# Two-layer diffusion trunk: a ninth ring slot, another order of the first loads, and the last expert scattered by itself

## The reference

```python
h  = x * (1.0 + sc1) + sh1                        # the context tokens the same, with their own rows
a, b, c, gates = split(h @ w_in[l])               # w_in: 1024 x 4768; three kinds of attention and their gates
y  = (g_a * (o_a @ w_branch_a) + g_b * (o_b @ w_branch_b) + g_c * (o_c @ w_branch_c)) @ w_out
x  = layer_norm(ALPHA * x + g1 * y, ln1_g, ln1_b)
h  = x * (1.0 + sc2) + sh2
aff = softmax(h @ w_router)                       # 16 experts, each takes its 32 best tokens of a stream
hid = silu(xs @ w_gate[e]) * (xs @ w_up[e])       # three 1024 x 1024 matrices for each expert
y  = zeros.at[chosen].add((hid @ w_down[e]) * top_aff)
x  = layer_norm(ALPHA * x + g2 * y, ln2_g, ln2_b)
```

## Time and profile before

| | |
|---|---|
| time, median of 3 runs | 1828.52 us (1828.32 to 1828.54) |
| the profiled execution | 1827.84 us |
| its span, first to last instruction | 1826.0 us |
| PE busy | 1556.5 us, 85% |
| DVE, ACT, GpSimd busy | 492.2, 396.0, 26.0 us |
| moved by DMA | 522.82 MB, mean 286 GB/s |
| mean granted TensorE clock | 0.921 |

### The profile page before, as it was taken

The page is one execution under the profiler, slowest core; times in us unless marked ns, Lnnn a source line. Parts: engine busy times, 40 slices in busy tenths (PEclk is TensorE's granted clock), DMA queues, the critical chain, the costliest instruction groups (busy, mean ns, idle before and its releaser), DMA issues.

```text
span 1826.0 us, 23042 instructions
## 1 busy us (share of the span) xinstructions
PE 1556.5 (85%) x9700; PEld 812.4 (44%) x9700; DVE 492.2 (27%) x1063; ACT 396.0 (22%) x889; POOL 26.0 (1%) x49
## 2 busy tenths in 40 slices
PE   5999999999998998988888899899977766666665
PEld 1444446888654442423222356468644323332222
DVE  0124786333342000111010243865340000000002
ACT  1212667221221120100000132674221100000000
POOL 1000000000000000000000010000000000000000
PEclk8999999999998999999999899999979767778876
DMA  9435911333529899999999711026869999999995
GB/s 373 176 144 225 352 64 70 98 98 130 211 113 398 327 422 422 421 421 420 421 422 421 300 45 41 24 81 209 313 263 421 420 421 421 421 421 420 420 421 239
DMA packets 98038, 522.82 MB, mean 286 GB/s; under 512 B 10752, under 2 KB 12944, under 8 KB 42640
## 3 DMA queue, kind: packets, MB, share of 16 engines
q1 hardware_dynamic: 94384, 510.44, 69.6%
q0 software_dynamic: 3392, 10.85, 1.7%
q10 hardware_dynamic: 160, 0.06, 0.0%
HBM read 520.17 MB, written 1.15 MB: 285 GB/s over the span
## 4 chain that ended last, share of the span: by engine, by line
PE 56%; DMA 35%; DVE 6%; ACT 1%; issue 1%; POOL 0%; DVEq 0%; SPq 0%; ACTq 0%
PE psum L443 53%; DMA ring<-in_w_up 21%; DMA ring<-in_w_down 12%; PE psum L493 3%; DMA ring<-in_w_in 2%; DVE small L1515 1%; DMA ring<-in_w_ada 1%; DVE PR L1535 1%; ACT hT L1081 0%; DVE X L1630 0%; DVE X L1547 0%; DVE psum L1513 0%; DVE X L1546 0%; DVE small L1517 0%; DVE stats L1636 0%
## 5 line engine op out<-in xcount | busy, mean ns | idle before, releaser
L443 PE MATMUL psum<-ring,A 128*32 128x256 f32 (+2 forms) x3176 | 494.4, 538 | 127.1 <-DMA ring<-in_w_up 65.3
L443 PEld LDWEIGHTS psum<-ring,A 128*32 128x32 f32 (+2 forms) x3176 | 167.1, 138 | 425.3 <-issue 186.2
L443 PE MATMUL psum<-ring,PR 128*32 128x256 f32 (+1 forms) x1440 | 187.3, 506 | 44.5 <-DMA ring<-in_w_down 44.2
L443 PE MATMUL psum<-ring_r,h_hi 128*128 128x512 f32 x576 | 178.6, 392 | 5.8 <-DVE h_lo L1703 5.8
L443 PE MATMUL psum<-ring,hT 128*128 128x512 f32 (+2 forms) x512 | 171.5, 489 | 11.0 <-DMA ring<-in_w_in 5.3
L1666 DVE TENSOR_TENSOR W<-W,psum 128x512 f32<-128x512 f32 (+1 forms) x32 | 17.8, 555 | 557.4 <-PE psum L443 557.4
L443 PEld LDWEIGHTS psum<-ring,PR 128*32 128x32 f32 (+1 forms) x1440 | 62.5, 129 | 163.0 <-issue 79.1
L443 PEld LDWEIGHTS psum<-ring,hT 128*128 128x128 f32 x512 | 86.1, 194 | 83.2 <-issue 83.2
L443 PEld LDWEIGHTS psum<-ring_r,h_hi 128*128 128x128 f32 x576 | 108.7, 189 | 29.2 <-issue 6.6
L443 PE MATMUL psum<-ring_r,h_lo 128*128 128x512 f32 x288 | 112.6, 391 | 0.0
L1300 ACT ACTIVATE W<-psum 128x512 f32<-128x512 f32 (+1 forms) x32 | 15.7, 490 | 444.8 <-PE psum L443 444.8
(11 more groups left out here) (181 smaller groups left out, 1326.0 us busy)
## 6 DMA issues: line engine op xcount, KB each, us to landing
ring<-in_w_gate SPq DMA_DIRECT2D x125, 1024.0 KB, 17.8
ring<-in_w_up SPq DMA_DIRECT2D x124, 1024.0 KB, 17.8
ring<-in_w_down SPq DMA_DIRECT2D x120, 1024.0 KB, 17.9
ring<-in_w_ada SPq DMA_DIRECT2D x48, 1024.0 KB, 11.7
ring<-in_w_in SPq DMA_DIRECT2D x36, 1024.0 KB, 5.1
ring<-in_w_out SPq DMA_DIRECT2D x8, 1024.0 KB, 7.0
ring<-in_w_branch SPq DMA_DIRECT2D x8, 768.0 KB, 4.5
A<-in_w_down SPq DMA_DIRECT2D x4, 1024.0 KB, 6.1
```

What stands on the lines that cost most here:

```text
L443: return nc.tensor.matmul(o, a, b, start=start, stop=stop, skip_group_check=True)
```

## The change

- `RING` is 9. The slot's 8 KB in each partition come from the scratch for descriptors of GpSimd's DMAs, which is set to 8192 bytes.
- Of the tables SP loads only the identity ahead of `w_ada`; ACT loads the rest after its first `ada_move`. GpSimd issues `x`, and with it the parameters, when slot 1 has been filled twice, which is when piece 10 has landed.
- The 16 experts are scattered in groups of 4, 4, 4, 3 and 1 (`SCATTERS`). The three, for all tiles, stand before `down(15)`, and the last one after it. In layer 0 tile 3 of the last scatter takes banks 6 and 7.
- The parameters of the projection get places in `PR` and `W` that are free after the last down, and GpSimd loads them for layer 1 then, before the layer norms. In layer 1 DVE does P(1,0) ahead of H(2), and P(1,0) takes a bank in turn.

```diff
-RING, SLOT = 8, 2048
+RING, SLOT = 9, 2048
...
-DVE_FIRST = [("H", 2), ("H", 3), ("P", 1, 0), ("P", 1, 1)]
+DVE_FIRST = [("P", 1, 0), ("H", 2), ("H", 3), ("P", 1, 1)]
...
-SCATTER_AT = {8: 0, 10: 1, 13: 2}
+SCATTER_AT = {8: 0, 10: 1, 13: 2, 16: 3}
+
+SCATTERS = [4, 4, 4, 3, 1]
+LAST_BANKS = (6, 7)
...
-        uq = part(PR, 0, 2, 384)
-        ukv = part(PR, 768, 512)
-        gain_cq = part(PR, 1280, 384)
-        gain_q = part(PR, 1664, HD)
-        gain_k = part(PR, 1728, HD)
-        bias_rows, cin = part(PR, 3584, P)[0:48 * DEPTH, :], part(PR, 3712, P)[0:2 * KT, :]
+        uq = part(PR, 2560, 2, 384)
+        ukv = part(W, 3584, 512)
+        gain_cq = part(PR, 3328, 384)
+        gain_q = part(PR, 3712, HD)
+        gain_k = part(PR, 3776, HD)
+        bias_rows, cin = part(A, 0, P)[0:48 * DEPTH, :], part(A, 128, P)[0:2 * KT, :]
...
-                        b = begin(("P", l, ch, t), takers=2 if ch != 0 else 1,
-                                  bank=ADA_BANK if l and (ch, t) == (1, 0) else None)
+                        b = begin(("P", l, ch, t), takers=2 if ch != 0 else 1)
...
                 def scatter(g):
-                    pe.wait_ge(y_ready, EXPERTS * l + 4 * g + 4)
+                    pe.wait_ge(y_ready, EXPERTS * l + 4 * g + SCATTERS[g])
...
                     for ts in ([0, 2], [1, 3]) if G == 2 else (tiles(l),):
                         banks = scatter_banks(g, ts)
-                        for j in range(4):
+                        for j in range(SCATTERS[g]):
                             scatter_rows(g, j, ts, banks)
...
-                    if e == EXPERTS:
-                        pe.wait_ge(y_ready, EXPERTS * l + e - 1)
-                        first = tiles(l)[:2]
-                        banks = scatter_banks(3, first)
-                        for j in range(3):
-                            scatter_rows(3, j, first, banks)
                     if e >= 1:
                         down(e - 1)
                     if e < EXPERTS:
                         turn_hidden(e)
-                pe.wait_ge(y_ready, EXPERTS * l + EXPERTS)
-                scatter_rows(3, 3, first, banks)
-                for t in tiles(l)[2:]:
-                    banks = scatter_banks(3, [t])
-                    for j in range(4):
-                        scatter_rows(3, j, [t], banks)
+                if G == 2:
+                    banks = scatter_banks(4, [0, 1, 2]) | scatter_banks(4, [3], LAST_BANKS)
+                    pe.wait_ge(y_ready, EXPERTS * l + EXPERTS)
+                    scatter_rows(4, 0, [0, 2], banks)
+                    scatter_rows(4, 0, [1, 3], banks)
+                else:
+                    banks = scatter_banks(4, tiles(l))
+                    pe.wait_ge(y_ready, EXPERTS * l + EXPERTS)
+                    scatter_rows(4, 0, tiles(l), banks)
...
-            sp.dma_start(cst[:, :], consts).then_inc(consts_in, 16)
+            sp.dma_start(ident, consts[:, C_ID:C_ID + P]).then_inc(consts_in, 16)
...
-            pool.wait_ge(slot_filled[3], 16)
+            pool.wait_ge(slot_filled[1], 32)
             pool.dma_start(X[:, 2:4, :], x.rearrange("b (t p) d -> p (b t) d", p=P)).then_inc(x_in, 16)
...
                 if l:
-                    pool.wait_ge(x_ready, 2 * first_tile(l))
-                    for t in tiles(l - 1):
-                        for n in (0, 1):
-                            filled(pool, ("SC", l - 1, 3, t, n))
...
+                    filled(pool, ("YE", l - 1, EXPERTS - 1))
+                pool.dma_start(gain_cq[:, 0:256], row(b_q_norm[l, :])).then_inc(proj_par_in, 16)
+                pool.dma_start(gain_cq[:, 256:384], row(b_kv_norm[l, :])).then_inc(proj_par_in, 16)
+                pool.dma_start(uq, b_w_uq[l].rearrange("(j p) n -> p j n", p=P)).then_inc(proj_par_in, 16)
+                pool.dma_start(ukv, b_w_ukv[l]).then_inc(proj_par_in, 16)
...
+                if l:
+
                     for t in tiles(l - 1):
                         for n in (0, 1):
-                            filled(pool, ("SC", l - 1, 3, t, n))
+                            filled(pool, ("SC", l - 1, 4, t, n))
...
             ada_move(0, 0)
+            act.dma_start(cst[:, C_MASK:C_ALL], consts[:, C_MASK:C_ALL]).then_inc(tables_in, 16)
...
-                    for i, t in enumerate((0, 1, 2, 3) if g == 3 else (0, 2, 1, 3)):
+                    for i, t in enumerate((0, 1, 2, 3) if g == 4 else (0, 2, 1, 3)):
...
-    nc = bacc.Bacc("TRN2", target_bir_lowering=False, num_devices=1)
+    nc = bacc.Bacc("TRN2", target_bir_lowering=False, num_devices=1,
+                   dynamic_dma_scratch_size=8192)
```

More of the change, by code:

```diff
@@ L201, in trunk @@
         consts_in = sem("consts_in")
+        tables_in = sem("tables_in")
         c_in = sem("c_in")
@@ L824, in scatter_rows @@
                 def scatter_rows(g, j, ts, banks):
-                    e = 4 * g + j
+                    e, last = 4 * g + j, j == SCATTERS[g] - 1
+                    e = e - (g == 4)
                     for i in sorted({t % 2 for t in ts}):
@@ L833, in scatter_rows, with scatter_banks @@
                             ins = mm(psum[:, b, at:at + Wd], ohT[e // 8][row:row + CAP, e % 8, i * P:(i + 1) * P],
-                                     ysb[row:row + CAP, e % 8, 0:Wd], j == 0 and at == 0, j == 3)
-                            if j == 3 and (G == 2 or i == 1):
+                                     ysb[row:row + CAP, e % 8, 0:Wd], j == 0 and at == 0, last)
+                            if last and (G == 2 or i == 1):
                                 end(ins, b)
-                def scatter_banks(g, ts):
+                def scatter_banks(g, ts, held=None):
                     if G == 2:
-                        return {(t, n): begin(("SC", l, g, t, n)) for t in ts for n in range(G)}
+                        return {(t, n): begin(("SC", l, g, t, n), bank=held and held[n]) for t in ts for n in range(G)}
                     opened = [begin(("SC", l, g, n)) for n in range(G)]
@@ L1004, in _ @@
                 if l:
-                    pool.wait_ge(x_ready, 2 * first_tile(l))
+                    filled(pool, ("YE", l - 1, EXPERTS - 1))
[3 more added lines that the diff above has]
+                pool.dma_start(ukv, b_w_ukv[l]).then_inc(proj_par_in, 16)
+                pool.dma_start(gain_q, row(c_q_norm[l, :])).then_inc(proj_par_in, 16)
+                pool.dma_start(gain_k, row(c_k_norm[l, :])).then_inc(proj_par_in, 16)
+                pool.dma_start(sink[:, :], row(a_sink[l, :])).then_inc(sink_in, 16)
+                pool.dma_start(wr[:, :, :], w_router[l].rearrange("(k p) e -> p k e", p=P)).then_inc(router_in, 16)
+                if l:
                     for t in tiles(l - 1):
                         for n in (0, 1):
-                            filled(pool, ("SC", l - 1, 3, t, n))
-                pool.dma_start(uq, b_w_uq[l].rearrange("(j p) n -> p j n", p=P)).then_inc(proj_par_in, 16)
-                pool.dma_start(ukv, b_w_ukv[l]).then_inc(proj_par_in, 16)
-                pool.dma_start(gain_cq[:, 0:256], row(b_q_norm[l, :])).then_inc(proj_par_in, 16)
-                pool.dma_start(gain_cq[:, 256:384], row(b_kv_norm[l, :])).then_inc(proj_par_in, 16)
-                pool.dma_start(part(PR, 1664, HD), row(c_q_norm[l, :])).then_inc(proj_par_in, 16)
-                pool.dma_start(part(PR, 1728, HD), row(c_k_norm[l, :])).then_inc(proj_par_in, 16)
-                pool.dma_start(sink[:, :], row(a_sink[l, :])).then_inc(sink_in, 16)
-                pool.dma_start(wr[:, :, :], w_router[l].rearrange("(k p) e -> p k e", p=P)).then_inc(router_in, 16)
+                            filled(pool, ("SC", l - 1, 4, t, n))
                 nc.gpsimd.memset(qpad[:, :, :], 0.0).then_inc(pads_zero, 1)
@@ L1425, in qkv @@
                         b = second(dve, ("P", l, 3, t))
+                        if l == 0 and t == 2:
+                            dve.wait_ge(tables_in, 16)
                         if t < 2:
@@ L1642, in scatter @@
                             add_rows(("SC", l, g, n), slice(2, 4), slice(Wd * n, Wd * n + Wd))
-                        if g == 3:
+                        if g == 4:
                             for n in range(G):
@@ L1681, in experts @@
                         mark(bank_drained[b])
-                scatter(3)
+                scatter(4)
             dve.wait_ge(consts_in, 16)
```

2 lines of the change are left out of this document (1 added, 1 removed).

## The result

The changed kernel takes **1814.26 us** (median of 4 runs, 1812.56 to 1817.42) against 1828.53 (4 runs, 1828.32 to 1831.56): a ratio of 0.993, 95% interval 0.9918 to 0.9942. The forecast was 1815.4, so it came out 1.1 us from the median. The profiled execution took 1814.61 us with a span of 1812.8; the span before was 1826.0, so the two traces differ by 13.2 us, and this is the difference to be explained. That the sum came out near does not say that its terms did.

A forecast was written before the change was run, and what follows sets the result against it. The weight stream bounds both expert stages, PE the stretches between. 5.1 + 1.35 + 2.49 + 1.7 + 2.49 = 13.1 us off 1827.84 gives 1814.7; the median adds 0.68: 1815.4 us, range 1811.5 to 1821.5.

The forecast's parts named there:

- The turn: Between the layers, end of down(14) to P(1,2) of layer 1: regrouped scatters gain 1.7 us.
- the start: First loads of layer 0: transposes of x begin at 44.3 instead of 49.40 us, gaining 5.1 us (bounds 3.1 to 6.4).
- New on the path is x: At the start: x issued at 34.2, taking 10.0 us, lands at 44.3; PE waits 1.3 us.
- The w_ada product: After the last P(1,t) at 79.93 us: with nine slots piece 16 comes earlier, removing PE's wait of 1.35 us.
- The ring slot: Expert stages of layers 0 and 1: one more piece landed at each standstill, each ending 2.49 us sooner.
- 24 matmuls ahead of down(15), so 5.42 us more: At the turn: with about 0.5 us for the fifth bank, down(15) ends 5.9 us later.
- The early parameters and the order of DVE: Layer 1's early parameter loads and P(1,0) ahead of H on DVE: 0 beyond the rest, gain bound 0.7 us.
- A: Start: x is not waited for, start gains 6.4 us, in all 14.4, 1814.1 us; chance 0.08.
- B: Turn: the 5.9 us ahead of y(15) stay, total gain 5.5 us, 1823.0 us; chance 0.10.
- C: Expert stages: the ring slot is worth nothing, total gain 8.1 us, 1820.4 us; chance 0.10.
- D: Halved descriptor scratch: GpSimd has one load in flight, N(0) 9.9 us late, gain 3.2, 1825.3 us; chance 0.06.
- E: Expert stages: nine pieces in flight slow the stream below 421 GB/s; 3% loss gives +11 us, 1839; chance 0.06.

The follow-up runs named there:

- The start alone: Kernel before (eight slots) with only the new order of the first loads, x after piece 10: 1827.97 us, ratio 1.0001.
- the slot alone: Kernel before with nine ring slots and the smaller descriptor scratch, nothing else: 1821.77 us, ratio 0.9971.
- The pairs by stream: Changed kernel with layer 0's last two scatters over tiles (0,1), then (2,3): 1824.22 us, repeated 1819.28 us.
- the turn alone: Changed kernel with eight slots and the old order of the first loads: 1821.48 us, ratio 0.9965.
- the seven slots: Kernel before with seven ring slots instead of eight: 1840.2 us, ratio 1.0069.
- the third series: Runs on another chip than the first two series, with the changed kernel unaltered (1814.64 us) beside others; kernel before 1827.49 us.

## Why the forecast came out, term by term

The sum was right and two of its terms were not. The turn gave 3.8 us more than said and the start 4.4 us less, and that these nearly cancelled is luck.

**The start, 5.1 us: failed.** Product 7 came at 26.38 (25.6 said) and P(1,0) at 32.13 (33.0 said), so the first half of the argument held. The step that failed is "New on the path is x", with the wait for x that it puts at 1.3 us. It has three parts. x was issued 1.4 us later than said, at 35.58. It took 11.4 us and not 10.0, so it landed at 47.0, later than the 46 named as a sign of error. And PE, after waiting 4.32 us, ran at half clock for a while, 1.7 us more, which was in no term. 0.72 us came out, below my lower bound of 3.1. The start alone, 0.3 us in its trace and no difference in time, shows it by itself, and x issued three pieces earlier gives 6.57 us more at P(1,2) and 5.25 us in time. The estimate of 4.4 us for this load, worked out from the unit cost in the Trainium skill, DMA: Bandwidth & Descriptors, in its section on the anatomy of a DMA on the gpsimd path, was farther off than the row. No run here shows it: the load took 9.5 to 14.7 us in every place it was tried, beside the weight stream.

**The w_ada product, 1.35 us: right.** 1.43 us in the trace, and the wait is gone with the slot alone too. In that trace, though, only 0.2 us are left of it at 634 us, as P(1,0) ran slower there (9.93 us, 9.01 before).

**The ring slot, 2.49 us twice: right.** 2.88 and 2.59 us in the traces; with the slot alone 3.06 and 2.52. Both of the figures of layer 0 are taken from 634 us on, at a product that PE does not wait for, and are the looser ones. The reading "one piece for each slot" holds from eight to nine slots. From seven to eight it holds in layer 1 (2.26) and not in layer 0 (1.16).

**The turn, 1.7 us: right in direction, mis-sized.** The term of the sum that failed is "24 matmuls ahead of down(15), so 5.42 us more". I took 5.42 us for 12 matmuls from the earlier trace rows, where both tiles use the same rows; in the changed order they take 2.86. So the 24 matmuls add 2 x 2.86 + 1.45 (the bank wait, 0.5 said) - 5.42 = 1.75 us ahead of down(15) and not 5.9. The row with the right order stood in the same trace, at 795.13: by it the term is 1.6 us. The error was to price the matmuls by their shape and not by the order of the tiles. The pairs by stream, which restore that price alone, put P(1,0) at T+32.31 and cost 4.6 us. The Trainium skill, TensorE: Matmul & The Clock Gate, in Part 3 on packing small matmuls, has matmuls of 32 rows (K=32) whose operands lie in different 32-row groups run at the same time, and gives 3.07 times the speed as measured for four. The trace agrees in kind: from two groups to four it is 5.42/2.86 = 1.9 times. No run here shows the 3.07.

**The early parameters and the order of DVE, 0 beyond the above: right as a sum, wrong as a reading.** In the kernel before, DVE did its half of H(2) first, at 1069.99, and its share of P(1,0) only at 1072.55, when the parameters had just landed (1071.2); P(1,0) to P(1,2) took 22.4 us there, much as after. In the changed kernel with late loads they landed 23.6 us behind the start of P(1,0), hardly later than before (22.1), but now H(2) stands behind DVE's share of P(1,0) and waits with it: this costs 3.3 us up to P(1,2), and some 6 in the times. So what covered the late loads was DVE's old order and not the length of the turn. The early loads are no gain of their own but the condition for the new order. Whether DVE's new order is needed by itself was not tried: with P(1,0) no longer in a bank of its own, H(3) waits for the bank that DVE's share of P(1,0) drains, and the old order would have DVE do H(3) before it.

**The rivals.** A (x is not waited for): refuted, 4.32 us. B (the turn costs 5.9): refuted by the turn alone, which gives 6.1. C (the slot gives nothing in the expert stages): refuted by the slot alone and by the seven slots. D (GpSimd held to one load): refuted; it issued its nine loads 0.52 to 0.73 us apart, as before, PE did not wait at N(0) (58.50 us), and the slot alone, with the smaller scratch, lost nothing. E (a slower stream): refuted, 421 and 416 GB/s as before.

**The better version.** Every part of the change with x issued behind piece 7 takes 1809.39 to 1809.55 us against 1814.26 and 1814.64 for the changed kernel, and beats both kernels. The 5.2 us under the changed kernel are from the third series, where both ran side by side.

## What to carry to other kernels

Where a load is moved behind others to let them pass, the moved load is the new last arrival. Of the three places tried here the best was right behind the one piece that must not be delayed; one piece earlier and three pieces later were both worse. A wait can cost more than its length, since PE may run at half clock behind it. A ring slot in front of a stage bound by its stream was worth about one piece from eight slots to nine, for each time the stream stood still before with a full ring; another step need not be worth the same. Take the price of small matmuls from a row with the same order over the groups of 32 rows, and look for it in the whole trace, not only at the place that changes. Ask of every "hidden" load whether its cover is an order of steps that the change turns round.

## What the runs showed of the hardware

- Twelve scatter matmuls (24 records of 32x512) take 5.42 us when they alternate between two groups of 32 rows and 2.86 us when they go over four, with the same bytes and the same count. Sixteen over four groups take 3.71 us. In the last scatter, 8 matmuls, either order takes 2.0 us.
- Some waits of PE were followed by a clock below 1.00, others not: behind 4.32, 6.08 and 3.50 us of waiting the same 16 records took 8.10, 8.38 and 8.71 us, where 7.03 to 7.10 is the time at full clock. Behind 0.55 us they took 7.03. The same wait has both outcomes: behind 2.64 us P(1,1) of layer 1 took 7.11 us in the changed kernel's first trace and 8.80 in its second (2.65 us of waiting).
- The same 1 MiB load took 12.0 us (kernel before), 11.4 (changed), 9.8 (start alone), 14.7 (behind piece 7) and 9.5 (behind piece 6), beside different pieces of the weight stream. Issued 2.7 us earlier (24.31 for 26.99) it was 5.2 us quicker, and it was then the w_in piece that came late. What decides which of the two goes ahead stays open.
- Runs of one kernel spread by some 5 us, as much as single parts of this change are worth, and the first 12 runs of the pairs by stream had a median 4.9 us above the five of its repetition. Half-clock stretches of PE do come and go between executions, but the mean granted clock of a run does not follow its time (0.921 for both 1823.62 and 1829.52 us), so the cause of the spread stays open.
